# The stick-breaking heads' query and key projections moved between the units of the joined attention

## The reference, cut to what matters

```python
def hybrid_mixer(x, w_in, ...):            # x: 512 x 1024
    h = split_columns(x @ w_in)
    y_a = mla_mixer(h['mla_cq'], h['mla_ckv'], h['mla_krope'], ...)      # 4 heads, low-rank q and kv
    y_b = nsa_mixer(h['nsa_q'], ...)       # compressed, selected and window attention, gated sum
    y_c = dsa_mixer(h['dsa_q'], h['dsa_k'], h['dsa_v'], h['idx_q'], h['idx_k'], h['idx_w'], ...)
    y_d = stick_breaking_mixer(h['sb_q'], h['sb_k'], h['sb_v'])
    y = concatenate([y_a, y_b, y_c, y_d])  # group norm, then @ w_out
def stick_breaking_mixer(q, k, v):         # 4 heads of 64, no rope
    z = q k^T * 64**-0.5;  mask = k_pos < q_pos
    log_1m = where(mask, log_sigmoid(-z), 0)
    after = reverse cumsum(log_1m) - log_1m
    return where(mask, exp(log_sigmoid(z) + after), 0) @ v
```

## Time and profile before

| | |
|---|---|
| median of 3 runs | 3371.89 us (3368.57 to 3374.22) |
| the profiled execution | 3378.78 us |
| its span | 3377.0 us |
| TensorE (PE) busy | 3249.0 us, 96% |
| DVE busy | 1492.9 us, 44% |
| ACT busy | 1271.5 us, 38% |
| POOL busy | 381.7 us, 11% |
| projections stage of layer 1, end | 1629.0 us |
| joined attention, layer 1 and layer 2 | 1629 to 1720, 2761 to 2856 us |

### The profile page before, as it was taken

How to read it: one execution, slowest core, us unless ns; L and a number is a source line. 1 busy time by engine, 2 the same in 40 slices (tenths; PEclk the granted TensorE clock), 3 DMA queues, 4 the chain that set the end, 5 groups by cost and what they waited for, 6 DMA issues and landing times. The chain is left out here.

```text
span 3377.0 us, 37327 instructions
## 1 busy us (share of the span) xinstructions
PE 3249.0 (96%) x14872; PEld 2571.8 (76%) x14872; DVE 1492.9 (44%) x2324; ACT 1271.5 (38%) x2190; POOL 381.7 (11%) x277
## 2 busy tenths in 40 slices
PE   8999999999999999999979999999999998899998
PEld 6867678878888888878656788878887766578886
DVE  4154522244243333344876433343334478663333
ACT  3344633234132223235655423242222456542222
POOL 0311324410000000003410000000000233000000
PEclk9998999999999999999999999999999999999999
DMA  4311213323333332323001223323332310023232
GB/s 147 94 44 38 88 57 100 99 88 94 99 94 97 97 100 94 99 97 100 14 1 63 88 94 94 100 88 94 99 94 82 129 43 1 26 81 100 94 94 75
DMA packets 76061, 276.92 MB, mean 82 GB/s; under 512 B 8688, under 2 KB 8944, under 8 KB 75632
## 3 DMA queue, kind: packets, MB, share of 16 engines
q1 hardware_dynamic: 75888, 274.54, 25.7%
HBM read 272.41 MB, written 2.10 MB: 81 GB/s over the span
## 5 line engine op out<-in xcount | busy, mean ns | idle before, releaser
L542 ACT ACTIVATE w_hi<-raw_slabs 128x1024 fp32r<-128x1024 f32 x489 | 516.4, 1057 | 1240.1 <-PE ps L582 1128.8
L557 DVE TENSOR_TENSOR w_lo<-raw_slabs,w_hi 128x1024 fp32r<-128x1024 f32 x372 | 454.8, 1224 | 721.8 <-ACT w_hi L542 721.7
L582 PE MATMUL ps<-in_hi,w_hi 128*128 128x512 f32 x1840 | 719.2, 391 | 6.9 <-DVE in_lo L907 5.1
L582 PE MATMUL ps<-in_lo,w_hi 128*128 128x512 f32 x1840 | 715.9, 389 | 0.0
L582 PE MATMUL ps<-in_hi,w_lo 128*128 128x512 f32 x1840 | 715.9, 389 | 0.0
L582 PE MATMUL ps<-parts,w_hi 128*128 128x512 f32 x2240 | 693.4, 391 | 0.9 <-DVE scratch L1524 0.8
L557 POOL TENSOR_TENSOR w_lo<-raw_slabs,w_hi 128x1024 fp32r<-128x1024 f32 x117 | 286.8, 2454 | 2366.5 <-ACT w_hi L542 2268.5
L582 PEld LDWEIGHTS ps<-parts,w_hi 128*128 128x128 f32 x2240 | 420.3, 188 | 92.5 <-issue 4.3
L582 PE MATMUL ps<-parts,w_lo 128*128 128x512 f32 x1120 | 435.9, 389 | 0.0
L582 PEld LDWEIGHTS ps<-in_hi,w_hi 128*128 128x128 f32 x1840 | 345.3, 188 | 86.0 <-DVE in_lo L907 9.2
L582 PEld LDWEIGHTS ps<-in_hi,w_lo 128*128 128x128 f32 x1840 | 345.4, 188 | 71.8
(11 more groups left out here) (288 smaller groups left out, 3525.3 us busy)
## 6 DMA issues: line engine op xcount, KB each, us to landing
raw_slabs<-weights SPq DMA_DIRECT2D x503, 512.0 KB, 3.5
big<-rope SPq DMA_DIRECT2D x2, 2304.0 KB, 8.8
x_resid<-xT SPq DMA_DIRECT2D x8, 256.0 KB, 4.2
outT<-x_resid SPq DMA_DIRECT2D x8, 256.0 KB, 2.0
const_cols<-consts SPq DMA_DIRECT2D x1, 836.0 KB, 9.1
scratch<-brow SPq DMA_DIRECT2D x1, 768.0 KB, 9.8
vector_cols<-vec SPq DMA_DIRECT2D x2, 45.5 KB, 9.5
vector_cols<-vec SPq DMA_DIRECT2D x1, 68.5 KB, 3.1
```

The source lines that it names most:

```text
L542: self.nc.scalar.activation(self.w_hi[:, m % SPLIT, :], self.raw[:, n % RAW, :], ACT.Copy)\
L557: (self.nc.gpsimd if i is None else self.nc.vector).tensor_tensor(self.w_lo[:, m % SPLIT, :], self.raw[:, n % RAW, :], self.w_hi[:, m % SP ...
L582: mm = k.nc.tensor.matmul(out, lhsT, rhs, start=(c == 0 and m == 0), stop=(last and m == 2))
```

## The change

- The jobs sk0, sk1, sq0, sq1 leave the projections stage. Their weights (four slabs) now stand behind the MLA weights and ahead of w_out. The MLA jobs are ordered four uq, then four uk.
- `SideJobs` does them in the joined attention: job j in units 12j to 12j+11, one weight tile (three matmuls of 512 columns) after the score of the units 2, 3, 4, 5, 7, 8, 9, 10 of each twelve, into bank 7; ACT makes up to slab +2 high parts at unit 3 of each twelve and evicts at unit 11; POOL makes one low part ahead of normalising units 0, 3, 6, 16, 28, 40 and splits the stick-breaking keys ahead of units 30 and 33. SyncE loads slabs in this phase.
- All weighted sums of the joined attention go to bank 6 (`outs=1`): the first pair of a group waits for the storing of the group before. The eight filler matmuls are gone there.
- x stays in place through the joined attention, so the NSA query halves move to `parts`, the outputs of MLA and NSA to tiles of `big`, and the late halves to the units 50, 54, 57, 60. Queries and keys of the stick-breaking heads get other tiles.
- `dense` is job 15 by the new numbers (uq3), so the NSA query halves stand beside the uk jobs.
- Block one: a high part between the second and the third square root; the wait for the first branch's halves one per tile (`wait_tile`) in place of one for all four; at `ROOTS + 3` one high part ahead of the last four high halves.

The core of the diff:

```diff
-            ("sk0", [(0, SK, P)]), ("sk1", [(0, SK + P, P)]), ("nq0", [(0, NQ, P)]), ("nq1", [(0, NQ + P, P)]),
-            ("dq0", [(0, DQ, P)]), ("dq1", [(0, DQ + P, P)]), ("sq0", [(0, SQ, P)]), ("sq1", [(0, SQ + P, P)]),
+            ("nq0", [(0, NQ, P)]), ("nq1", [(0, NQ + P, P)]), ("dq0", [(0, DQ, P)]), ("dq1", [(0, DQ + P, P)]),
...
         s.plain(v["uq"][0], len(s.tiles) - v["uq"][0])
+        for key, col in (("sk0", SK), ("sk1", SK + P), ("sq0", SQ), ("sq1", SQ + P)):
+            v[key] = s.columns("w_in_2", l, KD, [(0, col, P)])
...
-        if pair[0].first and pair[0].group >= 2:
-            pe.wait_ge(stored, k.at(stored, pair[0].group - 1))
-        weigh_pair(k, pair, [k.scr[:, 6 + i % 4, :] for i in (v - 1, v)], 6 + pair[0].group % 2).then_inc(pair_done, 1)
+        if pair[0].first and pair[0].group >= outs:
+            pe.wait_ge(stored, k.at(stored, pair[0].group - outs + 1))
+        weigh_pair(k, pair, [k.scr[:, 6 + i % 4, :] for i in (v - 1, v)], 6 + pair[0].group % outs).then_inc(pair_done, 1)
...
-                if paired and i == banks - 1:
+                if paired and not side and i == banks - 1:
                     k.keep_busy(pe, 8, bank=7)
-                advance(k, pe, i - lag, n, units, probs, probs_ready, turned, laid, unit_done, stored)
+                if side:
+                    side.tensor(pe, i)
+                advance(k, pe, i - lag, n, units, probs, probs_ready, turned, laid, unit_done, stored, **outs)
...
+                    if side:
+                        side.scalar(act, i)
...
+                for i in range(n):
+                    if side:
+                        side.gpsimd(pool, i)
+                    pool.wait_ge(row_inv, k.at(row_inv, i + 1))
+                    normalise(nc.gpsimd, i)
...
+            if j == 1:
+                ahead(1)
...
-            pe.wait_ge(s["lo_ready"], self.at("lo_ready", 4))
...
         if j == self.ROOTS + 3:
+            k.high_slabs(act, self.next_tile, 1)
...
+class SideJobs:
+    EACH, TILES, SPLIT_AT, TAKE_AT = 12, (2, 3, 4, 5, 7, 8, 9, 10), 3, 11
+    LOWS = (0, 3, 6, 16, 28, 40)
+    KEYS_AT = (30, 33)
...
+    def tensor(self, pe, i):
+        k = self.k
+        j, u = divmod(i, self.EACH)
+        if j >= len(self.jobs) or u not in self.TILES:
+            return
+        c = self.TILES.index(u)
+        tile = self.jobs[j][0] + c
+        k.need(pe, tile)
+        if j and c == 0:
+            pe.wait_ge(self.taken, k.at(self.taken, j))
+        for m, (lhsT, rhs) in enumerate(k.products(tile, self.x(c))):
+            mm = k.nc.tensor.matmul(k.ps[:, self.bank, :], lhsT, rhs, start=(c == 0 and m == 0),
+                                    stop=(c == KD - 1 and m == 2))
...
+        if u == self.SPLIT_AT:
+            k.high_slabs(act, at + KD - 1)
+        if u == self.TAKE_AT:
+            act.wait_ge(k.sums_done, self.ends[j])
+            k.nc.scalar.activation(out, k.ps[:, self.bank, :], ACT.Copy, scale=scale).then_inc(self.taken, 1)
+
+    def gpsimd(self, pool, i):
+        k = self.k
+        if i in self.LOWS:
+            k.low_slabs(pool, most=1)
+        if i in self.KEYS_AT:
...
-        pool.wait_ge(self.taken, k.at(self.taken, self.key_jobs))
...
-        self.keys.gpsimd(pool)
...
+        first_halves = {"wait_tile": lambda pe, c: pe.wait_ge(lo_ready, k.at(lo_ready, c + 1))} if d == 0 else {}
...
     for h in range(HEADS):
-        jobs.append(feature_job(k, lambda c: tile(6 + c), w["uq"][h], tile(25 + h), depth=2, split=False, rope="mq",
+        jobs.append(feature_job(k, lambda c: tile(6 + c), w["uq"][h], tile(21 + h), depth=2, split=False, rope="mq",
                                 scale=96 ** -0.5))
+    for h in range(HEADS):
         jobs.append(feature_job(k, lambda c: tile(8), w["uk"][h], tile(29 + h)[0:64], depth=1, split=False,
...
+    side = SideJobs(k, x, [(w["sk0"], tile(33), 1.0), (w["sk1"], tile(34), 1.0),
+                           (w["sq0"], tile(37), 64 ** -0.5), (w["sq1"], tile(38), 64 ** -0.5)], keys, 7)
     attention_phase(k, units, select, range(TOP_CUTS[0], TOP_CUTS[2]), paired=True, by_pool=True,
-                    lead=LateHalves(late, [40, 44, 48, 52]))
+                    lead=LateHalves(late, [50, 54, 57, 60]), side=side)
```

More of the change, by code:

```diff
@@ L657, in _ @@
                     pe.wait_ge(*signal)
-                for part, i, cols, start, stop in job["sum"]:
+                for c, (part, i, cols, start, stop) in enumerate(job["sum"]):
                     if i is not None:
                         k.need(pe, i)
+                    if "wait_tile" in job:
+                        job["wait_tile"](pe, c)
                     for m, (lhsT, rhs) in enumerate(part):
@@ L1905, in weigh_pair, with attend_pairs @@
     return mm
-def attend_pairs(k, pe, u, n, units, probs, ready, turned, laid, pair_done, stored):
+def attend_pairs(k, pe, u, n, units, probs, ready, turned, laid, pair_done, stored, outs=2):
     if 0 <= u < n:
@@ L1938, in lay_and_store_pairs @@
         act.wait_ge(pair_done, k.at(pair_done, w // 2 + 1))
-        nc.scalar.activation(units[w].out, k.ps[:, 6 + units[w].group % 2, 0:P], ACT.Copy).then_inc(stored, 1)
+        nc.scalar.activation(units[w].out, k.ps[:, 6 + units[w].group % outs, 0:P], ACT.Copy).then_inc(stored, 1)
 def attend(k, pe, u, n, units, probs, ready, turned, laid, unit_done, stored):
@@ L1973, in lay_and_store, with attention_phase @@
         nc.scalar.activation(one.out, k.ps[lo:hi, 5 + one.group % 3, 0:P], ACT.Copy).then_inc(stored, 1)
-def attention_phase(k, units, index=None, steps=range(0), lead=None, first=0, by_pool=False, lows=False, paired=False):
+def attention_phase(k, units, index=None, steps=range(0), lead=None, first=0, by_pool=False, lows=False, paired=False, side=None):
     nc = k.nc
@@ L2001, in attention_phase, with _ @@
     with k.block() as block:
+        if side:
+            @block.sync
+            def _(sp):
+                side.sync(sp)
         @block.tensor
@@ L2335, with __init__ @@
     ROOTS = 12
-    def __init__(self, k, gates, q, v, states, y, norm, halves, sums, out, taken, banks_free):
+    def __init__(self, k, gates, q, v, states, y, norm, halves, sums, out, taken, banks_free, next_tile):
+        self.next_tile = next_tile
         self.banks_free, self.gates_ready = banks_free, k.now("q_scaled")
@@ L2892, in passed @@
     def passed(self):
-        for part in (self.compress, self.norm, self.index, self.keys, self.halves):
+        for part in (self.compress, self.norm, self.index, self.halves):
             part.passed()
@@ L3143, in layer @@
     for key, i in at.items():
-        scale = 64 ** -0.5 if key in ("nq0", "nq1", "dq0", "dq1", "sq0", "sq1") else 1.0
+        scale = 64 ** -0.5 if key in ("nq0", "nq1", "dq0", "dq1") else 1.0
         jobs.append(feature_job(k, x, w[key], tile(i), rope=rope.get(key), scale=scale,
```

100 lines of the change are left out of this document (62 added, 38 removed).

## The result

The changed kernel takes **3379.94 us** (median of 16 runs, 3376.47 to 3390.26), and the kernel before, run beside it, 3371.86 us (16 runs, 3368.57 to 3380.28). The ratio is 1.0028, 95% interval 1.0019 to 1.0036. It is slower by 0.28%, where 0.28% faster was forecast; the time lies just inside the range, the sign is wrong. The profiled execution took 3390.26 us, with a span of 3388.5, 11.5 more than the 3377.0 of before.

A forecast was written before the change was run, and what follows sets the result against it. TensorE, 96% busy, was taken to bound the kernel, but DVE the joined attention. Terms -30.0 + 13.3 + 9.4 + 3.2 - 5.3 = -9.4 us against the median of 3371.9 gave 3362.5 us, range 3340 to 3380 (own range 3355 to 3369).

The forecast's parts named there:

- What bounds the kernel: Joined attention: DVE holds it, some 30 us of TensorE stand free; with side work TensorE becomes the bound in units 0 to 47.
- the price of the joined attention's first 48 units: TensorE's work of 66.3 us over DVE's share 0.906 gives 73.2 us: +13.3 and +9.4 in the two layers.
- The last 16 units: End of the joined attention: stays with DVE, gets two more late halves of 0.8 us, +1.6 us in each layer.
- The projections: Projections stage: four jobs leave, DVE's queue ends last, so 15 us shorter in each layer, not 21.8; both layers -30.0.
- POOL's interference: End of the projections: POOL's copies and key halves slow DVE's operations beside them by some 1.5 us in all.
- bounds of being right: Projections stage: the prediction is wrong if it ends less than 12 or more than 18 us sooner.
- Block one: Three small edits at TensorE's waits of 3.02, 3.35 and 1.85 us: -3.5 for the first two, -1.8 for the third, -5.3.
- B: Joined attention: one output bank, POOL's low parts and ACT's high parts lengthen the hand-over ring; +7.4 us, 3379; chance 0.17.
- A: Projections lose all 21.8 us, first 48 units run at TensorE's pace plus 3 us; -30.8 us, 3341; chance 0.15.
- C: Moved, not won: first 48 units at DVE's share 0.88, 75.3 us, block-one edits give nothing; 0, 3372; chance 0.25.

The follow-up runs named there:

- e3: Changed kernel plus 28 filler matmuls that no one reads, behind TensorE's last work in the projections stage; ratio 1.0011 to the kernel before.
- e6: Changed kernel with three score banks, side sums in bank 3 and two banks of weighed sums in the joined attention; 3372.77 us, ratio 0.9999.
- e12: Changed kernel with three score banks, two banks of weighed sums, and only one of each side tile's three products computed (not exact); 3355.51 us, ratio 0.9949.
- e9: Kernel before with its four late halves of the queries at units 50, 54, 57, 60 instead of 40, 44, 48, 52; ratio 1.0000.
- e1: Kernel before with only the change's three edits in block one; 3368.72 us beside 3377.64, ratio 0.9983.
- e5: Changed kernel with GpSimd's low parts in the joined attention cut to 8 columns (not exact); ratio 1.0004 to the kernel before.
- e13: Kernel before with three score banks instead of four in the joined attention, two banks of weighed sums kept; ratio 1.0003.

## Why the prediction was wrong

**What bounds the kernel** was read rightly: TensorE became the bound of the first 48 units, and DVE's busy time there is unchanged at 52.7 us.

**The step that failed most is the price of the joined attention's first 48 units**, 66.3/0.906 = 73.2 us, which put the clock at the stage's start at nothing, and the wait for the one bank of sums at nothing beyond the share. They measured 77.4 and 77.7, 8.7 us more in two layers. The runs put it down as follows.
- The start at half clock. I forecast that TensorE would stand idle ahead of the stage and gave the clock behind that no price. It is at half for the first 7.4 and 8.0 us. That costs 2.4 us in layer 1, by e3; layer 2 was never run at full clock, and I can only estimate as much for its like stretch.
- The one bank of sums. It costs 1.4 us in layer 1, by e6, and up to 2.2 in layer 2.

That is 3.8 of the 4.2 us in layer 1, and by the estimate about 4 of the 4.5 in layer 2. It is not good to a tenth: before's own two layers take 59.9 and 63.8 us.

With full clock and two banks, then, some 73.6 us are left (75.0 less 1.4), and the 73.2 comes out. I take that for luck, since both of its parts are off. The work is more than 66.3 us, as starts in after's middle show:

```profile
1655.06 0.88 PE L1907 MATMUL ps<-scratch,big 128*64 128x128 f32 x12
1655.87 0.74 PE L1882 MATMUL ps<-parts 128*128 128x512 f32 x2
...
1656.50 0.44 PE L2799 MATMUL ps<-in_hi,w_hi 128*128 128x512 f32 x1
1656.78 0.39 PE L2799 MATMUL ps<-in_lo,w_hi 128*128 128x512 f32 x1
1657.01 0.39 PE L2799 MATMUL ps<-in_hi,w_lo 128*128 128x512 f32 x1
1657.24 0.38 PE L1890 MATMUL ps<-const_cols,scratch 128*128 128x128 f32 x2
```

Twelve records of weighed sums take 0.81 us, 0.068 each and not 0.053 (204 of them: 3 us), and a side tile 0.74 and not 0.68 (32: 2 us). So an estimate of TensorE's work is 71 us, and the share that it reaches nearer 0.96 than 0.906, which was read off DVE, in a middle where nothing was added. The two errors cancel here and not in general: by the same formula a third of the side load would leave TensorE at (66.3 - 14.5)/0.906 = 57.2 us, below what the stage takes without any, and e12 took 65 (about 63 without its start at half clock).

**The last 16 units**: +2.6 and +1.5 against +1.6 each. The sum nearly agrees for a wrong reason: the two more late halves cost nothing (e9), the bank costs 3.0 and 2.4 (e6).

**The projections**: -12.1 us in layer 1, not -15. The mechanism was as told (DVE last, by ropes and query halves; the four query halves at 2.84 us as forecast). The mis-sized term is POOL's interference: I gave 1.5 us for it in all. In the rows above three index additions beside POOL's copies take 3.79 us, three free of them 2.44; the rope steps at 1597.75, 1598.88, 1604.09 and 1605.28 take 1.09, 0.98, 1.15 and 1.64 us where the last tile's take 0.68 and 0.69. That is 1.35 + 0.41 + 0.29 + 0.47 + 0.95 = 3.5 us, 2.0 more than I gave. Another 0.3 is that the first row maximum came 1.15 us after the stage's last work, at half clock (0.8 in before, behind ACT's), and 0.5 is my own rounding: 1629.0 less 1614.5 is 14.5, not 15. The Trainium skill, "SBUF — State Buffer", section Who interferes with whom, says that a DVE instruction with two SBUF inputs contends with a GpSimd instruction that reads SBUF; the trace agrees (1.64 us beside POOL's L2755, 0.69 without). In layer 2 the stretch from the stage's first eviction to the first row maximum is 12.8 us shorter (125.2 to 112.4), and 2.9 of it was lost ahead of that eviction (8.8 us from the stage's opening, 5.9 in before), in a half-clock stretch that before does not have there and that no term of mine covered:

```profile
2633.80:2640.60 6.80, 6.19 (x15) 4.87 (x16) 0.28 (x1) 1.06 (x1) 2.37 (x1) 0.50 0.65 211
```

The 9.9 us of layer 2 are outside the 12 to 18 that I had named as bounds of being right; the 77.4 and 77.7 us above are just within theirs.

**Block one**: -3.6 us, not -5.3 (e1: -3.2). The second and third gap went as told (3.35 to 3.44 us in parts with TensorE's work between, 1.85 to none), but the first kept 1.82 of its 3.02 us. Half clock did not go, it moved: 3.4 us at each of the first two gaps in before, one stretch of 6.8 us (411.7 to 418.5) in after.

**The rivals.** B's place and mechanism was in part the true one: it named the one bank, and gave the break-even for the first 48 units as 77.9 us with full gains elsewhere. The units stopped just short of it, and the projections and block one brought 9.7 us less than the 35.3 it counted on (12.1 + 9.9 + 3.6 = 25.6). Either alone would have taken the forecast's -9.4 to about nothing (-0.7 with the units' 8.7, +0.3 with the 9.7); only both together turned the sign. B had 0.17. POOL's low parts, which B named too, cost nothing (e5). A fell: DVE's tail is real, and the half-clock time that it hoped to see go grew from 80 to 123 us. C's 75.3 us was nearer than my 73.2, but its share of 0.88 was read over a stretch that was partly at half clock (0.94), so it may have been near for that reason.

**What stays open.** What layer 2 takes with a start at full clock, and why the clock fell there in e3 although TensorE was busy. Whether the first third of the side load is as dear as the rest. Where the -1.8 us behind layer 1's joined attention and the +1.3 at the end come from.

## What to carry to other kernels

Before work is moved into a stage "because the engine is free there", price one piece of it: fill the stage with a third of the load and then with all, and read the slope. Here two thirds of the 0.227 us of an added matmul were paid, though the engine had seemed a third free. Ask also what the emptied place does to TensorE's clock: the 7 us that it stands idle at the end of the projections are followed by 7 to 8 us at half clock in the next stage. When a PSUM bank has to be given up, give up last the one whose owner waits in order behind a slow reader: a fourth score bank was worth nothing that could be measured, the second accumulator some 12 us. And when a repaired version wins, take off what its unrelated edits win alone.

## What the hardware showed beside this

TensorE can be put to half clock while no idle time of it is recorded. The stretch of before and of e13 from 260 to 280 us, at the same place of the same program:

```profile
260.00:280.00 20.00, 20.00 (x65) 12.43 (x65) 5.49 (x21) 5.41 (x20) 0.00 (x0) 0.59 0.00 1
```

```profile
260.00:280.00 20.00, 20.00 (x104) 12.44 (x104) 9.32 (x35) 9.44 (x34) 0.00 (x0) 1.00 0.00 1
```

The first is before's, the second e13's. Busy for 20.00 of 20.00 us in both, it was granted 0.59 in one and 1.00 in the other, and did 65 matmuls against 104; from 240 to 300 us before's trace has no wait of TensorE at all. The stretch is 17.1 us long, so an execution with it is some 8.5 us longer, nearly all that this change was forecast to win. What decides whether it comes is not shown: seven of the fourteen traces have it, before's and after's among them, and all edits lie behind it in the program. The "TensorE: Matmul & The Clock Gate" page of the Trainium skill, section What's actually happening, lets activity release the throttle; at this place a busy engine was throttled all the same.
